# The first feed-forward's gate and up products in the 512-column form that the second one has

## The chip, the core and the metric

The kernel runs on one core of a Trainium2 chip, in one launch. Its time is the time of that core in microseconds (us): the median of three runs was 1943.56 us (1940.8 to 1944.72). The engines: TensorE (PE in the profile; PEld is its weight load), VectorE (DVE), ScalarE (ACT), GpSimd (POOL), and SyncE (SP), which issues the transfers.

## The reference, cut to what matters

The program is a four-layer model on 256 tokens with 1024 features in float32. Only the feed-forward of the first layer is touched. With `x` the normed and modulated hidden state (256 tokens by 1024), it computes

```python
a = silu(x @ w_gate) * (x @ w_up)      # 1024 -> 2816 (FFN_HIDDEN), twice
y = a @ w_down                         # 2816 -> 1024
```

and the second layer's feed-forward is the same with other weights.

## The kernel before, in words

Precision. Each float32 operand is cut into a high part (rounded to fp32r, a copy by ScalarE) and a low part (the operand minus its high part, by VectorE or GpSimd). A product is the sum of three: high times high, high weight times low x, low weight times high x. x lies transposed as `hH` and `hL`, 8 tiles of 128 features by 256 tokens; the two stand side by side in the tensor `hpair`, and `hP[:, k]` is tile k of both, 512 columns.

The weight stream. All weights come in slabs of 128 x 2048, in the order of `weight_order`; for a feed-forward that is gate i, up i, down i-1, for i from 0 to 10. SyncE loads slabs into three places of `raw`. A slab is two blocks of 1024 columns (8 weight tiles of 128 x 128). For block j, ScalarE writes the high part (`cut_hi`, L2603) and VectorE or GpSimd the low part (`cut_lo`, L1512) into a ring of three blocks, so the high cut of a block waits until TensorE has used the block three before it. In a feed-forward the blocks alternate between VectorE and GpSimd (`lo_engine`: `("V", "G")[j % 2]`). By the number that the blocks have, VectorE has the first half of each slab and GpSimd the second in the first feed-forward (its first gate slab and its last down slab have places of their own), and it is the other way round in the second.

One round i of a feed-forward (`pe_ffn`, `ve_ffn`, `se_ffn`, `ge_ffn`), each engine in its own fixed order of instructions:

- TensorE: gate i (16 tiles), up i (16 tiles), down i-1 (24 matmuls of 512 columns). In the first feed-forward a tile is three matmuls of 256 columns (`pe_mm3`, L603 to L605), and both halves of the hidden tile pair share one PSUM bank. In the second it is `pe_mm2`: one matmul of 512 columns, high weight against `hP[:, k]` (L615), and one of 256, low weight against `hH` (L616); each half of the pair has a bank of its own, with the x-high product in columns 0 to 255 and the x-low product in 256 to 511.
- ScalarE: the high cuts of the blocks that come next; `Silu` of gate i; after VectorE's product the high part of the activation (`chi`, L2924); further high cuts.
- VectorE: the low cuts; `act = silu(gate) * up` (first feed-forward L1987, reading up from PSUM; second L2014, both inputs in SBUF); the low part of the activation (`clo`, L1990). In the second feed-forward it first adds the two 256-column halves of each bank with a `tensor_reduce` (`ve_halves`, L1549), four per round.
- TensorE's down i needs chi and clo of round i; it comes one whole round later, but for down 10, which stands right behind down 9.

The modulation in pieces. The matrix of the next modulations is computed by VectorE from a stream of its own, one piece of the list `ADA` at a time: `ve_ada` is two operations over 128 x 512 (L1541, or L1538 and L1541 at the first of four), and after each fourth piece TensorE sums over partitions (`pe_ada`, L824) and VectorE copies the result (L1530). A piece stands ahead of every gate and every up, on both engines, and one more behind the activation of rounds 2, 4, 6 and 8 of the first feed-forward (`FFN_PIECES`). On TensorE, the `pe_ada` that sums waits until VectorE has finished the piece before it. In the first feed-forward TensorE's sums stand ahead of gate 1, down 1 (round 2), up 4, gate 6, up 7 and gate 9.

Of the kernel before, what the change touches and what calls it, by code (L numbers as in the profile page):

```python
# [553 lines left out]
class Net:  # L554
# [490 lines left out]
    def pe_ffn(self, e, layer):  # L1045
        m = self.m
        self.P.mark("end", f"mixer{layer}", "P")
        self.pe_norm(e, f"ffn{layer}")
        for i in range(11):
            if i == 0:  # L1050
                self.banks.order = ACC
            if layer:
                self.pe_linear_halves(e, "w_gate1", i, None if i else "ffn1")
                self.banks.order = ROT
                self.pe_linear_halves(e, "w_up1", i)
            else:
                self.pe_linear(e, "w_gate0", i, 8, 2, m.hH, m.hL, None if i else "ffn0")
                self.banks.order = ROT
                self.pe_linear(e, "w_up0", i, 8, 2, m.hH, m.hL)
            if i:  # L1060
                if layer == 0 and i in FFN_PIECES:
                    self.pe_ada(e)
                if i == 10:
                    self.pe_gate_rows(e, f"ffn{layer}_post", layer, 5)
                self.pe_down(e, layer, i - 1)
        if layer == 0:
            self.pe_ada_until(e, 1, 1)
        self.pe_down(e, layer, 10)
# [900 lines left out]
    def ve_ffn(self, e, layer):  # L1969
# [5 lines left out]
        for i in range(11):  # L1975
            s = slice(2 * (i % 2), 2 * (i % 2) + 2)
            if i == 10:
                self.ve_gate_rows(e, f"ffn{layer}_post", layer, 5, f"g_ffn_post{layer}")
            if layer:
                self.ve_act_halves(e, i)  # L1980
            else:
                self.ve_linear(e, "w_gate0", i, 8, 2, first=i == 0)
                self.ve_linear(e, "w_up0", i, 8, 2)
                e.wait_ge(*self.at("out", "w_gate0", i))
                e.wait_ge(*self.at("full", "w_up0", i))
                pu = self.banks.tile("w_up0", i)[:, 0:512].rearrange("p (a t) -> p a t", a=2)
                e.tensor_tensor(out=m.act[:, s, :], in0=m.act[:, s, :], in1=pu, op=ALU.mult).then_inc(  # L1987
                    *V(("act", 0, i), ("out", "w_up0", i)))
            e.wait_ge(*self.at("hi", f"act{layer}", i))
            e.tensor_tensor(out=m.cL[:, s, :], in0=m.act[:, s, :], in1=m.cH[:, s, :].bitcast(F32), op=ALU.subtract).then_inc(  # L1990
                *V(("lo", f"act{layer}", i)))
            if i:
                if layer == 0 and i in FFN_PIECES:
                    self.ve_ada(e)
                self.ve_cuts(e, f"w_down{layer}", 16 * i - 1)
# [2 lines left out]
        self.cut_lo(e, V, self.W.last(f"w_down{layer}", 16 * 11 - 1) + 1)  # L1998
        self.ve_junction(e, f"ffn{layer}_post", ("mix1", "mix2")[layer])

    def ve_act_halves(self, e, i):

        m, V = self.m, self.V
        s = 2 * (i % 2)
        self.ve_linear(e, "w_gate1", i, 8, 2, first=i == 0)
        for j in range(2):
            self.ve_halves(e, m.act[:, s + j, :], "w_gate1", i, j)
        self.ve_linear(e, "w_up1", i, 8, 2)
        for j in range(2):
            self.ve_halves(e, m.up[:, j, :], "w_up1", i, j)  # L2010
        e.wait_ge(*V.last)
        self.cut_lo(e, V, self.W.last("w_up1", 16 * i + 15) + 3)
        e.wait_ge(*self.at("silu", 1, i))
        e.tensor_tensor(out=m.act[:, s:s + 2, :], in0=m.act[:, s:s + 2, :], in1=m.up, op=ALU.mult).then_inc(*V(("act", 1, i)))  # L2014

    def ve_mix1(self, e):
        m, V = self.m, self.V
# [881 lines left out]
    def se_ffn(self, e, layer):  # L2899
# [6 lines left out]
        for i in range(11):  # L2906
            s = slice(2 * (i % 2), 2 * (i % 2) + 2)
            self.se_linear(e, f"w_gate{layer}", i, 8, 2)
            if layer:
                self.cut_hi(e, self.W.last("w_up1", 16 * i + 15) + 1)  # L2910
                e.wait_ge(*self.at("out", "w_gate1", i, 1))
                e.activation(m.act[:, s, :], m.act[:, s, :], ACT.Silu, scale=1.0).then_inc(*A(("silu", 1, i)))
                self.cut_hi(e, self.W.last("w_up1", 16 * i + 15) + 3)
            else:
                self.se_linear(e, "w_up0", i, 8, 2)
                e.wait_ge(*self.at("full", "w_gate0", i))
                if i >= 2:
                    e.wait_ge(*self.at("lo", "act0", i - 2))
                e.activation(m.act[:, s, :], self.banks.tile("w_gate0", i)[:, :].rearrange("p (a t) -> p a t", a=2),
                             ACT.Silu, scale=1.0).then_inc(*A(("out", "w_gate0", i)))  # L2920
            e.wait_ge(*self.at("act", layer, i))
            if i >= 2:
                e.wait_ge(*self.at("down", layer, i - 2))
            e.activation(m.cH[:, s, :], m.act[:, s, :], ACT.Copy, scale=1.0).then_inc(*A(("hi", f"act{layer}", i)))  # L2924
            if i:
                self.se_cuts(e, f"w_down{layer}", 16 * i - 1)
# [710 lines left out]
```

## Time and profile before

| | value |
|---|---|
| median of three runs | 1943.56 us |
| the profiled execution's own time | 1943.31 us |
| its span | 1941.1 us |
| TensorE busy | 1867.3 us, 96% of the span |
| VectorE busy | 1442.8 us, 74% |
| ScalarE busy | 991.3 us, 51% |
| GpSimd busy | 257.8 us, 13% |
| transfer of a piece (`ada`), from issue to landing | 4.7 us |
| granted TensorE clock, mean over the span | 0.995 |
| first feed-forward, from its first gate matmul on | from 234.5 us |
| second feed-forward, the same | from 663.5 us |

The profile is of one execution. "Busy" is the time in which an engine has at least one instruction under way. Matmuls overlap in their pipeline, so the time of a stream of matmuls is read from the distance of their starts and not from their durations.

### The profile page before, as it was taken

To read this page: it belongs to the slowest core of one execution; us is meant where nothing else is said; L and a number is where in the kernel's file an instruction comes from. 1 tells how busy PE (TensorE), PEld (TensorE's weight loads), DVE (VectorE), ACT (ScalarE), POOL (GpSimd) and SP (SyncE) were. 2 spreads that over 40 slices of the span, in tenths; PEclk is the share of its full clock that TensorE was granted. 3 is DMA by queue.
4 is the path that set the end of the run, shared out by engine and by line. 5 is a ranking of instruction groups with operands and counts; after the bars stand their busy time and mean duration, and the time that the engine had idled before them with its cause. 6 is when DMAs were issued, how large, how long until landed. Compare 5 with 4: busy or idle time off the path is not lost.

```text
span 1941.1 us, 31807 instructions
## 1 busy us (share of the span) xinstructions
PE 1867.3 (96%) x12460; PEld 1688.7 (87%) x12460; DVE 1442.8 (74%) x2603; ACT 991.3 (51%) x1428; POOL 257.8 (13%) x118
## 2 busy tenths in 40 slices
PE   6999999999998999999999899999999999999998
PEld 5987799999987788889988899999988888888887
DVE  5898875568769775567666579888878887777776
ACT  5655544455455644465555555666643334444444
POOL 0001044430001244420000373000000000000000
PEclk9999999999999999999999999999999999999999
DMA  8763476756574365555344344677766765464452
GB/s 318 241 217 135 149 265 249 259 205 232 181 256 165 123 229 179 191 178 206 143 159 168 120 163 163 200 215 216 217 240 249 281 239 217 179 249 180 186 205 109
DMA packets 94548, 391.89 MB, mean 202 GB/s; under 512 B 7680, under 2 KB 41776, under 8 KB 56000
## 3 DMA queue, kind: packets, MB, share of 16 engines
q1 hardware_dynamic: 94112, 389.59, 56.7%
q8 instruction: 100, 1.64, 0.3%
q14 instruction: 48, 0.39, 0.1%
q10 hardware_dynamic: 288, 0.26, 0.0%
HBM read 371.74 MB, written 15.73 MB: 200 GB/s over the span
## 4 chain that ended last, share of the span: by engine, by line
PE 75%; DVE 14%; ACT 2%; issue 2%; DMA 1%; POOL 0%; DVEq 0%; ACTq 0%
PE ps L615 9%; PE acc L599 9%; PE acc L601 9%; PE acc L600 9%; PE ps L616 5%; PE ps L603 5%; PE ps L604 5%; PE ps L605 5%; PE acc L603 3%; PE acc L604 3%; PE acc L605 3%; DVE wlo L1512 2%; DVE arena L1541 2%; PE acc L1467 1%; PE ps L1467 1%
## 5 line engine op out<-in xcount | busy, mean ns | idle before, releaser
L2603 ACT ACTIVATE whi<-raw 128x1024 fp32r<-128x1024 f32 x553 | 584.2, 1059 | 427.4 <-PE acc L601 206.1
L1512 DVE TENSOR_TENSOR wlo<-raw,whi 128x1024 fp32r<-128x1024 f32 x457 | 556.3, 1224 | 276.0 <-ACT whi L2603 275.6
L1512 POOL TENSOR_TENSOR wlo<-raw,whi 128x1024 fp32r<-128x1024 f32 x96 | 240.0, 2503 | 605.5 <-ACT whi L2603 605.2
L599 PE MATMUL acc<-whi,chi 128*128 128x512 f32 x744 | 293.9, 395 | 4.3 <-DVE wlo L1512 1.9
L601 PE MATMUL acc<-wlo,chi 128*128 128x512 f32 x744 | 291.2, 391 | 0.0
L600 PE MATMUL acc<-whi,clo 128*128 128x512 f32 x744 | 290.5, 390 | 0.0
L615 PE MATMUL ps<-hpair,whi 128*128 128x512 f32 x784 | 278.8, 397 | 1.4 <-POOL wlo L1512 1.4
L603 PE MATMUL ps<-hpair,whi 128*128 128x256 f32 x912 | 262.8, 288 | 4.3 <-DVE wlo L1512 3.1
L604 PE MATMUL ps<-hpair,whi 128*128 128x256 f32 x912 | 258.6, 284 | 0.0
L605 PE MATMUL ps<-hpair,wlo 128*128 128x256 f32 x912 | 258.5, 283 | 0.0
L616 PE MATMUL ps<-hpair,wlo 128*128 128x256 f32 x784 | 219.8, 280 | 0.0
L603 PE MATMUL acc<-hpair,whi 128*128 128x256 f32 x712 | 205.3, 288 | 4.3 <-DVE wlo L1512 3.6
L604 PE MATMUL acc<-hpair,whi 128*128 128x256 f32 x712 | 201.3, 283 | 0.0
L605 PE MATMUL acc<-hpair,wlo 128*128 128x256 f32 x712 | 201.3, 283 | 0.0
L603 PEld LDWEIGHTS ps<-hpair,whi 128*128 128x128 f32 x912 | 175.4, 192 | 6.4 <-issue 2.6
L615 PEld LDWEIGHTS ps<-hpair,whi 128*128 128x128 f32 x784 | 147.3, 188 | 36.9 <-issue 1.6
L604 PEld LDWEIGHTS ps<-hpair,whi 128*128 128x128 f32 x912 | 175.5, 192 | 0.3
L605 PEld LDWEIGHTS ps<-hpair,wlo 128*128 128x128 f32 x912 | 175.3, 192 | 0.0
L599 PEld LDWEIGHTS acc<-whi,chi 128*128 128x128 f32 x744 | 140.1, 188 | 36.0 <-issue 2.7
L601 PEld LDWEIGHTS acc<-wlo,chi 128*128 128x128 f32 x744 | 139.9, 188 | 31.6
L600 PEld LDWEIGHTS acc<-whi,clo 128*128 128x128 f32 x744 | 140.3, 189 | 26.8
L616 PEld LDWEIGHTS ps<-hpair,wlo 128*128 128x128 f32 x784 | 147.9, 189 | 2.5
(509 smaller groups left out, 3101.4 us busy)
## 6 DMA issues: line engine op xcount, KB each, us to landing
raw<-in_peer_down SPq DMA_DIRECT2D x64, 1024.0 KB, 4.9
raw<-in_peer_up SPq DMA_DIRECT2D x64, 1024.0 KB, 5.0
arena<-in_ada SPq DMA_DIRECT2D x80, 512.0 KB, 4.7
raw<-in_w_gate SPq DMA_DIRECT2D x22, 1024.0 KB, 4.8
raw<-in_w_up SPq DMA_DIRECT2D x22, 1024.0 KB, 4.9
raw<-in_w_down SPq DMA_DIRECT2D x22, 1024.0 KB, 4.8
arena<-spill SPq DMA_DIRECT2D x14, 1024.0 KB, 6.8
spill<-hT_t SPq DMA_DIRECT2D x22, 448.0 KB, 6.3
```

Of the source, the lines that this page charges most:

```text
L599: e.matmul(out, xh, hi, start=start, stop=False, skip_group_check=True)
L600: e.matmul(out, xl, hi, start=False, stop=False, skip_group_check=True)
L601: i = e.matmul(out, xh, lo, start=False, stop=stop, skip_group_check=True)
L603: e.matmul(out, hi, xh, start=start, stop=False, skip_group_check=True)
L604: e.matmul(out, hi, xl, start=False, stop=False, skip_group_check=True)
L605: i = e.matmul(out, lo, xh, start=False, stop=stop, skip_group_check=True)
L615: e.matmul(ps.rearrange("p (s t) -> p s t", s=2), hi, self.m.hP[:, k], start=k == 0, stop=False, skip_group_check=True)
L616: i = e.matmul(ps[:, 0:T], lo, self.m.hH[:, k, :], start=False, stop=k == 7, skip_group_check=True)
L1467: t = e.matmul(ps[:, i * 128:(i + 1) * 128], m.oh1[:, n % 3, i * 128:(i + 1) * 128], m.oh2[n % 3][:, i * 128:(i + 1) * 128], start=True, s ...
L1512: e.tensor_tensor(out=lo, in0=w, in1=hi.bitcast(F32), op=ALU.subtract).then_inc(*X(("lo", j)))
L1541: e.scalar_tensor_tensor(out=m.ada_acc, in0=w, scalar=c, in1=m.ada_acc, op0=ALU.mult, op1=ALU.add).then_inc(*V(*([("ada", s)] if k else [])))
L2603: e.activation(hi, w, ACT.Copy, scale=1.0).then_inc(*self.A(("hi", j)))
```

## The change

The first feed-forward takes the second's form. In `pe_ffn` both layers call `pe_linear_halves`. VectorE's `ve_act_halves` gets the layer as an argument: per round it adds the two gate banks into `act`, does its piece and its low cuts, adds the two up banks into `up`, makes the low cuts up to three blocks past up's last one (before: two, and no cut between up's sum and the product), waits for ScalarE's Silu, and multiplies `act` by `up`, both in SBUF. ScalarE cuts high parts up to one block past up's last, then waits for VectorE's sum of the gate, applies Silu in SBUF, cuts two blocks more, and waits for the product.

```diff
@@ pe_ffn
-            if layer:
-                self.pe_linear_halves(e, "w_gate1", i, None if i else "ffn1")
-                self.banks.order = ROT
-                self.pe_linear_halves(e, "w_up1", i)
-            else:
-                self.pe_linear(e, "w_gate0", i, 8, 2, m.hH, m.hL, None if i else "ffn0")
-                self.banks.order = ROT
-                self.pe_linear(e, "w_up0", i, 8, 2, m.hH, m.hL)
+            self.pe_linear_halves(e, f"w_gate{layer}", i, None if i else f"ffn{layer}")
+            self.banks.order = ROT
+            self.pe_linear_halves(e, f"w_up{layer}", i)
@@ ve_ffn
-            if layer:
-                self.ve_act_halves(e, i)
-            else:
-                self.ve_linear(e, "w_gate0", i, 8, 2, first=i == 0)
-                self.ve_linear(e, "w_up0", i, 8, 2)
-                e.wait_ge(*self.at("out", "w_gate0", i))
-                e.wait_ge(*self.at("full", "w_up0", i))
-                pu = self.banks.tile("w_up0", i)[:, 0:512].rearrange("p (a t) -> p a t", a=2)
-                e.tensor_tensor(out=m.act[:, s, :], in0=m.act[:, s, :], in1=pu, op=ALU.mult).then_inc(
-                    *V(("act", 0, i), ("out", "w_up0", i)))
+            self.ve_act_halves(e, layer, i)
@@ ve_act_halves, with the layer for the 1 in every name
+        self.ve_linear(e, f"w_gate{layer}", i, 8, 2, first=i == 0)
         for j in range(2):
+            self.ve_halves(e, m.act[:, s + j, :], f"w_gate{layer}", i, j)
+        self.ve_linear(e, f"w_up{layer}", i, 8, 2)
         for j in range(2):
+            self.ve_halves(e, m.up[:, j, :], f"w_up{layer}", i, j)
+        e.wait_ge(*V.last)
+        self.cut_lo(e, V, self.W.last(f"w_up{layer}", 16 * i + 15) + 3)
+        e.wait_ge(*self.at("silu", layer, i))
+        e.tensor_tensor(out=m.act[:, s:s + 2, :], in0=m.act[:, s:s + 2, :], in1=m.up, op=ALU.mult).then_inc(*V(("act", layer, i)))
@@ se_ffn
-            if layer:
-                self.cut_hi(e, self.W.last("w_up1", 16 * i + 15) + 1)
-                e.wait_ge(*self.at("out", "w_gate1", i, 1))
-                e.activation(m.act[:, s, :], m.act[:, s, :], ACT.Silu, scale=1.0).then_inc(*A(("silu", 1, i)))
-                self.cut_hi(e, self.W.last("w_up1", 16 * i + 15) + 3)
-            else:
-                self.se_linear(e, "w_up0", i, 8, 2)
-                e.wait_ge(*self.at("full", "w_gate0", i))
-                if i >= 2:
-                    e.wait_ge(*self.at("lo", "act0", i - 2))
-                e.activation(m.act[:, s, :], self.banks.tile("w_gate0", i)[:, :].rearrange("p (a t) -> p a t", a=2),
-                             ACT.Silu, scale=1.0).then_inc(*A(("out", "w_gate0", i)))
+            self.cut_hi(e, self.W.last(f"w_up{layer}", 16 * i + 15) + 1)
+            e.wait_ge(*self.at("out", f"w_gate{layer}", i, 1))
+            e.activation(m.act[:, s, :], m.act[:, s, :], ACT.Silu, scale=1.0).then_inc(*A(("silu", layer, i)))
+            self.cut_hi(e, self.W.last(f"w_up{layer}", 16 * i + 15) + 3)
```

## Rows read from the trace of the kernel before

**Rows 1.** The page: the chain that ended last, by engine.

```profile
PE 75%; DVE 14%; ACT 2%; issue 2%; DMA 1%; POOL 0%; DVEq 0%; ACTq 0%
```

**Rows 2.** Windows: length, PE, PEld, DVE, ACT, POOL busy (instructions), clock, DMA share, GB/s.

```profile
250.03:419.39 169.36, 169.29 (x1221) 160.51 (x1220) 103.48 (x105) 71.60 (x78) 74.71 (x29) 1.00 0.72 259
679.64:842.60 162.96, 162.96 (x869) 139.51 (x869) 97.68 (x100) 72.25 (x78) 70.51 (x29) 1.00 0.56 198
```

**Rows 3.** Timeline of PE: start, us, engine, line, operation; ends of two gapless streams.

```profile
338.27 0.28 PE L603 MATMUL ps<-hpair,whi 128*128 128x256 f32 x1
...
343.55 0.28 PE L605 MATMUL ps<-hpair,wlo 128*128 128x256 f32 x1
...
747.07 0.40 PE L615 MATMUL ps<-hpair,whi 128*128 128x512 f32 x1
...
755.91 0.40 PE L615 MATMUL ps<-hpair,whi 128*128 128x512 f32 x1
```

**Rows 4.** Timeline, all engines, around the activation of round 8, first feed-forward.

```profile
384.54 0.69 DVE L1987 TENSOR_TENSOR arena<-arena,ps 128x512 f32<-128x512 f32 x1 [3.45 <-PE ps L605]
385.26 0.63 ACT L2924 ACTIVATE chi<-arena 128x512 fp32r<-128x512 f32 x1 [2.07 <-DVE arena L1987]
385.80 1.05 ACT L2603 ACTIVATE whi<-raw 128x1024 fp32r<-128x1024 f32 x1
385.93 0.69 DVE L1990 TENSOR_TENSOR clo<-arena,chi 128x512 fp32r<-128x512 f32 x1 [0.70 <-ACT chi L2924]
386.73 1.54 DVE L1541 SCALAR_TENSOR_TENSOR arena<-arena,gs_t 128x512 f32<-128x512 f32 x2
387.28 1.06 ACT L2603 ACTIVATE whi<-raw 128x1024 fp32r<-128x1024 f32 x1 [0.43 <-PE acc L601]
388.42 3.22 POOL L1512 TENSOR_TENSOR wlo<-raw,whi 128x1024 fp32r<-128x1024 f32 x1 [3.22 <-ACT whi L2603]
389.74 1.05 PE L824 MATMUL ps<-kc_t,arena 128*128 128x128 f32 x8
390.00 1.06 ACT L2603 ACTIVATE whi<-raw 128x1024 fp32r<-128x1024 f32 x1 [1.66 <-PE acc L601]
```

**Rows 5.** Timeline of DVE and POOL: a piece that meets a GpSimd cut.

```profile
300.65 3.56 DVE L1541 SCALAR_TENSOR_TENSOR arena<-arena,gs_t 128x512 f32<-128x512 f32 x2
300.86 2.80 POOL L1512 TENSOR_TENSOR wlo<-raw,whi 128x1024 fp32r<-128x1024 f32 x1 [3.22 <-ACT whi L2603]
```

**Rows 6.** Timeline of the first feed-forward's start: DVE, POOL, ACT, PE.

```profile
241.63 7.34 DVE L1541 SCALAR_TENSOR_TENSOR arena<-arena,gs_t 128x512 f32<-128x512 f32 x4
246.02 2.40 POOL L1512 TENSOR_TENSOR wlo<-raw,whi 128x1024 fp32r<-128x1024 f32 x1 [0.60 <-ACT whi L2603]
244.88 1.06 ACT L2603 ACTIVATE whi<-raw 128x1024 fp32r<-128x1024 f32 x1 [1.07 <-PE ps L605]
245.47 0.38 PE L603 MATMUL ps<-hpair,whi 128*128 128x256 f32 x1 [0.69 <-POOL wlo L1512]
249.02 1.16 PE L824 MATMUL ps<-kc_t,arena 128*128 128x128 f32 x8 [0.42 <-DVE arena L1541]
```

**Rows 7.** Timeline of the first feed-forward's end: last product, cuts, down 9, down 10.

```profile
419.12 1.03 PE L769 MATMUL ps<-kc_t,gs_t 128*128 128x128 f32 x8
420.65 1.04 ACT L2603 ACTIVATE whi<-raw 128x1024 fp32r<-128x1024 f32 x1
421.73 1.23 DVE L1512 TENSOR_TENSOR wlo<-raw,whi 128x1024 fp32r<-128x1024 f32 x1 [0.26 <-ACT whi L2603]
422.87 1.22 DVE L1512 TENSOR_TENSOR clo<-raw,chi 128x1024 fp32r<-128x1024 f32 x1
424.15 0.50 PE L599 MATMUL acc<-chi 128*128 128x512 f32 x1
```

**Rows 8.** The second feed-forward: a pair of sums, and a product that meets GpSimd.

```profile
678.33 1.28 DVE L1549 TENSOR_REDUCE arena<-ps 128x256 f32<-128x512 f32 x2
679.64 2.57 DVE L2014 TENSOR_TENSOR arena<-arena 128x512 f32<-128x512 f32 x1
```

More of the change, by code:

```diff
@@ L1999, in ve_ffn, with ve_act_halves @@
         self.ve_junction(e, f"ffn{layer}_post", ("mix1", "mix2")[layer])
-    def ve_act_halves(self, e, i):
+    def ve_act_halves(self, e, layer, i):
         m, V = self.m, self.V
         s = 2 * (i % 2)
-        self.ve_linear(e, "w_gate1", i, 8, 2, first=i == 0)
+        self.ve_linear(e, f"w_gate{layer}", i, 8, 2, first=i == 0)
         for j in range(2):
-            self.ve_halves(e, m.act[:, s + j, :], "w_gate1", i, j)
-        self.ve_linear(e, "w_up1", i, 8, 2)
+            self.ve_halves(e, m.act[:, s + j, :], f"w_gate{layer}", i, j)
+        self.ve_linear(e, f"w_up{layer}", i, 8, 2)
         for j in range(2):
-            self.ve_halves(e, m.up[:, j, :], "w_up1", i, j)
+            self.ve_halves(e, m.up[:, j, :], f"w_up{layer}", i, j)
         e.wait_ge(*V.last)
-        self.cut_lo(e, V, self.W.last("w_up1", 16 * i + 15) + 3)
-        e.wait_ge(*self.at("silu", 1, i))
-        e.tensor_tensor(out=m.act[:, s:s + 2, :], in0=m.act[:, s:s + 2, :], in1=m.up, op=ALU.mult).then_inc(*V(("act", 1, i)))
+        self.cut_lo(e, V, self.W.last(f"w_up{layer}", 16 * i + 15) + 3)
+        e.wait_ge(*self.at("silu", layer, i))
+        e.tensor_tensor(out=m.act[:, s:s + 2, :], in0=m.act[:, s:s + 2, :], in1=m.up, op=ALU.mult).then_inc(*V(("act", layer, i)))
     def ve_mix1(self, e):
```

## The prediction

> **What bounds the kernel now.** I read the chain of waits first: TensorE holds 75% of what ended last [rows 1]. Then the windows from the first product of each feed-forward to its last [rows 2]: in the first one TensorE is busy for 169.29 of 169.36 us, so the stage is as long as its matmuls. Whatever VectorE gets to do is free until a wait of TensorE appears, and a saving is worth what it takes out of TensorE's stream. The second feed-forward, which has the new form, needs 162.96 us for the same work. That gap of 6.4 us is not the gain: besides cheaper tiles, the first holds sums of the modulation (L824), five in its window, which stay (1.05 us long each, 389.74 in [rows 4]; 4 to 5 us in all). So the distances of matmul starts come next [rows 3], and last the timelines of one round, of the start and of the end [rows 4 to 7], to see which waits the new order makes.
>
> **Matmuls removed and added.** Before, from 338.27 to 343.55 there are 44 steps of 256 columns: 0.1200 us each, 0.3600 us a tile. In the second feed-forward, from 747.07 to 755.91 there are 25 tiles of 512 + 256 columns: 0.3536 us each [rows 3]. The columns are the same 768; one instruction and one weight load go. Each tile saves 0.0064 us. Of 11 x 32 = 352 tiles, the 16 of gate 0 go through `pe_first`, with the same matmuls in both forms; 336 x 0.0064 = 2.15 us saved. Bounds: 1.7 to 2.2, the lower one from the windows [rows 2], where what is left after the down matmuls and sums is about 0.360 against 0.355 us a tile.
>
> The Trainium skill ("TensorE: Matmul & The Clock Gate", Back-to-back issue gap) gives the isolated gap at full clock as N / 2.4 + 2.5 ns, so that one instruction less saves 2.5 ns a tile, an estimate of 0.84 us over 336 tiles. The rows show 6.4 ns, and a step of 256 columns 11 ns longer than that formula's; the sum by it would be 1.3 us later.
>
> **VectorE's additions.** Four reduces a round at 0.64 us (1.28 for two, [rows 8]) are 2.56 us, 28 us in all. The window shows VectorE busy 103.5 of 169.4 us, so there is room; the price lies only where somebody waits for it. Below, U is the start of the first matmul behind up (the product L1987 starts at U + 0.27; in round 8 U = 384.27), and T' the start of the next gate, or of a sum ahead of it: 389.74, so U + 5.47 [rows 4].
>
> In round i the new order on VectorE behind U is: second reduce of up at U + 0.27 to 0.95; then the low cut of the next gate's first half, which now stands before the product. ScalarE's high cut of that block can start when up's last block is used, U + 0.26 (as 390.00 follows 389.74), and VectorE's low cut starts 1.08 behind a high cut's start (420.65 to 421.73), so U + 1.34; the product follows 1.14 later (421.73 to 422.87), U + 2.48. That is 2.2 us later than today. The rest keeps the steps of [rows 4]: chi 0.72 behind (U + 3.20), clo 0.67 behind chi (3.87), ScalarE's high cut of the next gate's second half 0.54 behind chi (3.74), GpSimd's low cut of it 1.14 behind (4.88), and a piece of the modulation 0.80 behind clo (4.67). Nobody on TensorE waits for chi and clo, but for round 10. GpSimd's cut, 2.80 us when a piece meets it [rows 5], ends at U + 7.7. TensorE wants it 2.83 behind T' (8 tiles), at U + 8.3 less a load ahead: 0.45 us to spare. I cost it at nothing; if the cover goes, see the second rival.
>
> What meets what: an L1541 that is issued while GpSimd cuts ends 0.55 us behind GpSimd (300.65 + 3.56 = 304.21 against 300.86 + 2.80 = 303.66, [rows 5]). The first operation of the piece starts at 4.67, ahead of GpSimd; the second is caught and ends at 7.68 + 0.55 = U + 8.23. Today in round 8 the piece runs 386.73 to 388.27, ahead of GpSimd's 388.42 [rows 4].
>
> - Rounds 2, 4, 6, 8 have a piece behind the activation. Behind round 8's, TensorE's sum ahead of gate 9 waits for exactly that piece (`pe_ada` waits for the piece before). It could start at U + 5.47 and gets it at U + 8.29: **2.8 us of new stall**, once. The other sums have a piece before them that was done long before: in round 2 and at up 4 and up 7 half a slab's tiles or more earlier, at gate 6 the piece of up 5.
> - Rounds 4 and 6: the gate's own piece follows, 1.54 us for two operations [rows 4], then the low cut of the next up's first half (1.22 us), from 8.23 + 1.54 = U + 9.8 to 11.0. TensorE wants it at T' + 5.66 less a load ahead, U + 11.0. Together 0.2 us lost; bounds 0 and 2, the latter if each slips by a sum's length. In round 2 TensorE's own sum shifts T' by up to 1 us and there is room.
> - Bank waits: gate and up now take four banks of four a round; each is needed again a round later, and its reduce is done in U + 0.95 at the latest. Nothing, lower bound and upper.
> - Transfers: slabs free with the low cuts; GpSimd's, which frees the gate slab, comes 0.7 us later (U + 4.88 against 388.42 - 384.27 = 4.15), against a slab every 5.5 us or so. The pieces' own transfers wait for VectorE two pieces back and take 4.7 us; ahead of up 5 and up 7 VectorE may wait for one until about 1 us later, with 0.9 us of room behind. Nothing, up to 1 us.
>
> **The start.** Today TensorE's sum ahead of gate 1 waits 0.42 us in its row and some more before: up 0 restarts at 245.47 and needs 16 - 8 = 8 tiles, to 248.3, but the sum starts at 249.02, because the fourth L1541 was issued at 246.00, just as GpSimd took 246.02 to 248.42 [rows 6]. In the new order ScalarE does Silu (after two operations of the piece, 241.63 + 1.54, two reduces, to 244.4, and a table load that ends about 245.1) before the high cut that is at 244.88 today; the cut moves to about 245.6, GpSimd to 246.75, and the L1541 gets through by 246.75. **0.7 us saved**, bounds 0 (caught again) and 0.7.
>
> **The end.** Down 10 stands right behind down 9, and its last weight block has a place in `chi`'s memory: high cut behind chi, low cut behind clo. Today the matmul that uses it starts at 424.15, U + 5.03, right behind that low cut (422.87 + 1.22 = 424.09, [rows 7]). Now chi is at U + 3.20, the high cut of the spare at 3.74, the low cut at 4.82 to 6.04; the matmul at U + 6.1: **1.05 us lost**, not covered by anything, since the junction behind it waits for the accumulators. Bounds 0.7 and 2.4, the latter if the product is caught by GpSimd.
>
> **Sum.** -2.15 - 0.7 + 2.8 + 0.2 + 1.05 = +1.2 us. On the profiled execution's own 1943.31 us (span 1941.1 and 2.2 around it) that is 1944.5. That execution is 0.25 us under the median 1943.56, so for a median I write 1944.7. The gain in the stream is real and is spent on three waits.
>
> **Rivals.**
> 1. *No new stall*: GpSimd's cut is later or the piece sooner, so the sum ahead of gate 9 finds its piece done, and the end costs little. For it: the second feed-forward does run gapless in this form [rows 2]; against: there, but for the first two rounds, no pieces are left, and it is GpSimd that has the next gate's first half, so that VectorE's product comes 1 us behind U. Time: 1943.6 - 2.15 - 0.7 = 1940.7.
> 2. *GpSimd's cut misses the gate's second half every round.* The new product has both inputs in SBUF and took 2.57 us with GpSimd busy, against 0.69 [rows 8, 4]. If in each round it is caught at U + 2.5, chi and GpSimd's next cut come up to 1.9 us later, which passes the 0.45 us of room: 1.4 us in each of 9 rounds, 13 us, 1956. It decides from the point where GpSimd is still cutting at U + 2.5. Against: GpSimd's cut before that follows the use of up's first half, U - 2.83 + 0.26 + 1.14 = U - 1.4, and takes 2.4 [rows 6], so it ends at U + 1.0. The Trainium skill ("SBUF — State Buffer", Who interferes with whom) says that a VectorE instruction with two SBUF inputs and a GpSimd one that reads SBUF exclude each other for the whole instruction, and a `tensor_reduce` never contends; the trace agrees (2.57 us for the product, reduces at 0.64 beside GpSimd). By that rule alone every product would be exposed that was not before, with the time just given.
> 3. *Rounds 4 and 6 (and the transfers of pieces) slip as well*: +2 to 3 us more, 1947.
>
> **How the numbers follow.** Forecast 60% (its own range 1943 to 1946.5), rival 1 20%, rival 2 (in whole or in part, 1948 to 1957) 12%, rival 3 8%. 0.2% is 3.9 us, about what a measurement of this kernel can tell from no change: faster means below 1939.7, slower above 1947.4. Faster takes savings at their upper bounds, no stall, and 1 us besides: 5%. Slower: rival 2 and a third of rival 3: 15%. The rest, 80%, is no change. The range leaves out rival 2 and a part of rival 1: 1940.5 to 1948.5.
>
> **What would show it.** In the changed kernel's profile: L615 and L616 at 0.3536 us a tile in the first stage; no L1987; L2014 about 2.5 us behind the first down matmul in rounds 1 to 9, at 0.69 us; L824 ahead of gate 9 with an idle of TensorE of about 2.8 us before it, released by L1541; L824 ahead of gate 1 with none; the spare block's matmul about 6.1 us behind the last up matmul. Wrong would be: TensorE idle ahead of the second half of gates (rival 2), or no idle at gate 9 (rival 1).

## The result, and the profile after

The change costs 0.46%: 1950.96 us (six runs, 1948.38 to 1953.25) against 1941.52 us (six runs, 1939.65 to 1944.72), a ratio of 1.0046 with a 95% interval of 1.0034 to 1.0057. The forecast was 1944.7 us, with a range up to 1948.5; it was +1.2 us on the median of three then known (1943.56), against +9.4 us here. The profiled execution of the changed kernel took 1953.25 us, its span 1951.4 us. In the rows below, line numbers before L1512 are unchanged, `cut_lo` is now L1507, `ve_ada` L1536, `ve_halves` L1544, `clo` L1976, the product L2000, `cut_hi` L2589, `chi` L2902 and Silu L2897.

The page after: the chain that ended last by engine, the gate and up matmuls among its costliest groups (busy us, mean ns of one | idle ahead of them, and what ended most of it), and the busy times of the engines.

```profile
PE 75%; DVE 14%; ACT 3%; issue 2%; DMA 1%; POOL 0%; DVEq 0%; ACTq 0%; SPq 0%
...
L615 PE MATMUL ps<-hpair,whi 128*128 128x512 f32 x1120 | 401.0, 400 | 5.6 <-DVE wlo L1507 3.4
...
PE 1870.0 (96%) x12124; PEld 1672.6 (86%) x12124; DVE 1469.1 (75%) x2647; ACT 992.1 (51%) x1428; POOL 256.9 (13%) x118
```

By engine, the chain stands almost as it did [rows 1]. The difference is in the idle: 5.6 us ahead of L615, most of it released by a low cut of VectorE. The window from the first product to the last of the first feed-forward, with the columns of [rows 2], puts it in place:

```profile
250.21:427.41 177.20, 171.18 (x903) 146.22 (x902) 131.22 (x146) 72.36 (x78) 73.58 (x29) 0.98 0.67 245
```

In the window of the first feed-forward TensorE now idles 177.20 - 171.18 = 6.02 us, where it idled 0.07 us, and the granted clock is 0.98. Whoever waited for whom is in the waits of TensorE between 234 and 450 us (total, times, longest):

```profile
PE ps L615 <- DVE wlo L1507: 3.4, 2, 2.1
PE ps L824 <- DVE arena L1536: 2.6, 1, 2.6
PE acc L599 <- ACT chi L2902: 1.0, 1, 1.0
PE ps L615 <- POOL wlo L1507: 0.9, 1, 0.9
```

The stage, from the first transpose (L757) of the norm ahead of this feed-forward to the first of the norm behind it, is 202.93 us before and 210.81 after: +7.88 us. To see which rounds pay, I cut the stage where the down products begin: the first matmul of L599 behind up i (for round 10 that is 0.8 us behind U below, since eight matmuls of L769 stand between). "1" is from the start of the stage to the first down matmul of round 1, the other numbers are from the first down matmul of the round before, so that "5" has gate 5 and up 5 in it, and "end" is from that of round 10 to the end of the stage. In every row the parts add up to the stage, but for rounding.

```
us            1      2      3      4      5      6      7      8      9      10     end    stage
before        29.96  17.79  17.08  17.87  16.98  17.87  17.86  16.98  17.87  17.77  14.90  202.93
after         28.72  17.81  16.85  17.58  20.61  17.46  19.14  16.76  22.17  17.58  16.13  210.81
e1            29.14  17.60  16.86  17.58  16.76  17.50  21.80  16.75  18.84  17.58  17.21  207.62
e2            28.74  17.65  16.85  17.58  17.58  17.44  18.43  16.76  17.50  17.56  16.13  202.22
e3            28.72  17.80  16.86  17.58  19.12  17.46  19.14  16.74  17.58  21.63  16.13  208.77
e4            28.75  17.65  16.83  17.58  19.14  17.44  19.05  16.76  22.86  17.56  16.13  209.73
e5            28.78  17.60  16.86  17.58  16.76  17.50  17.56  16.76  19.26  17.55  14.77  200.97
e6            28.56  17.57  16.86  17.58  16.76  17.50  17.56  16.76  17.50  17.56  14.72  198.91
e7            28.71  17.81  16.85  17.58  20.64  17.46  19.04  16.77  20.62  17.55  16.13  209.17
```

An undisturbed round without a sum (round 8) is 16.76 us now and was 16.98: 0.22 us less, the price of 32 tiles at 0.0069 us. Rounds 5, 7 and 9 are 3.6, 1.3 and 4.3 us longer than before, and the end 1.2 us. Round 9 and the end are what the prediction named; rounds 5 and 7 it had at 0.2 us together.

A text written ahead of a run that names a step from one activation to the next takes it from `clo` to `clo`; so measured, round 9 of the changed kernel is 22.53 us. Where `clo` itself moves within its round the two measures differ, by up to 2.7 us.

**Round 9.** The timeline around the activation of round 8, all engines, as [rows 4]:

```profile
387.30 1.23 DVE L1507 TENSOR_TENSOR wlo<-raw,whi 128x1024 fp32r<-128x1024 f32 x1 [0.53 <-ACT whi L2589]
388.45 0.69 DVE L2000 TENSOR_TENSOR arena<-arena 128x512 f32<-128x512 f32 x1
...
389.83 0.69 DVE L1976 TENSOR_TENSOR clo<-arena,chi 128x512 fp32r<-128x512 f32 x1 [0.70 <-ACT chi L2902]
390.63 3.50 DVE L1536 SCALAR_TENSOR_TENSOR arena<-arena,gs_t 128x512 f32<-128x512 f32 x2
390.83 2.76 POOL L1507 TENSOR_TENSOR wlo<-raw,whi 128x1024 fp32r<-128x1024 f32 x1 [3.98 <-ACT whi L2589]
...
394.19 1.65 PE L824 MATMUL ps<-kc_t,arena 128*128 128x128 f32 x8 [2.65 <-DVE arena L1536]
```

The last up matmul before it is followed by down at 385.88 (U). The cut now stands ahead of the product (387.30, 388.45), so `clo` is at U + 3.95 and the piece at U + 4.75, 0.20 us ahead of GpSimd's cut. Its second operation is caught, meaning that it was issued while GpSimd was cutting and ended only behind that cut: the piece ends at 394.13, 0.54 us behind GpSimd, and TensorE's sum starts at U + 8.31, forecast at U + 8.29.

**Rounds 5 and 7.** The timeline of gate 5, DVE, POOL and PE:

```profile
311.92 0.39 PE L599 MATMUL acc<-whi,chi 128*128 128x512 f32 x1
...
316.66 5.19 DVE L1536 SCALAR_TENSOR_TENSOR arena<-arena,gs_t 128x512 f32<-128x512 f32 x4
321.59 2.50 POOL L1507 TENSOR_TENSOR wlo<-raw,whi 128x1024 fp32r<-128x1024 f32 x1 [1.93 <-ACT whi L2589]
321.77 3.40 DVE L1507 TENSOR_TENSOR wlo<-raw,whi 128x1024 fp32r<-128x1024 f32 x1
325.31 0.47 PE L615 MATMUL ps<-hpair,whi 128*128 128x512 f32 x1 [2.13 <-DVE wlo L1507]
```

The first row is the first matmul behind up 4, so U = 311.92. Two pieces run back to back (4 operations, 5.19 us). Between U and the end of the cut VectorE's waits are put down to up's last matmul, ScalarE's high cut and `chi`, none to a transfer. VectorE's low cut of up's first half is issued behind them, 0.18 us after GpSimd took its own cut, and lasts 3.40 us instead of 1.22: it ends 1.08 us behind GpSimd, and TensorE, which wants it for the first tile of up 5, stands for 2.13 us. In the kernel before, the same cut was issued at 323.22, 1.10 us ahead of GpSimd:

```profile
323.22 1.22 DVE L1512 TENSOR_TENSOR wlo<-raw,whi 128x1024 fp32r<-128x1024 f32 x1
...
324.32 2.40 POOL L1512 TENSOR_TENSOR wlo<-raw,whi 128x1024 fp32r<-128x1024 f32 x1 [2.35 <-ACT whi L2603]
```

Gate 7 has the same pair of rows again in the changed kernel (3.40 us issued at 359.85, GpSimd at 359.67), with an idle of 1.24 us; there TensorE still has the sum ahead of up 7 to do.

**The clock.** Windows of 2 us behind gate 5's stall and gate 9's (columns as above; the clock is the number ahead of the last two):

```profile
325.00:327.00 2.00, 1.69 (x8) 1.49 (x9) 1.90 (x4) 0.60 (x1) 0.00 (x0) 0.86 1.05 389
327.00:329.00 2.00, 2.00 (x8) 1.71 (x7) 1.96 (x3) 0.03 (x1) 0.00 (x0) 0.50 1.01 426
329.00:331.00 2.00, 2.00 (x10) 1.75 (x10) 0.83 (x2) 1.05 (x1) 0.00 (x0) 0.79 0.09 37
...
395.00:397.00 2.00, 2.00 (x9) 1.81 (x9) 1.09 (x3) 0.00 (x0) 0.00 (x0) 0.50 0.95 324
397.00:399.00 2.00, 2.00 (x10) 1.71 (x10) 1.36 (x2) 0.00 (x0) 0.00 (x0) 0.72 1.04 434
```

After TensorE had stood still, the granted clock went from 1.00 to 0.50 (2.4 to 1.2 GHz) for about 3.4 us, although TensorE was busy again. A window at 0.50 holds 8 or 9 matmuls; the same tiles at 1.00 are 14 (the second window of e7 below). Time times missing share is 1.7 us for each fall. This is not in the prediction's sum at all.

**Start and end.** The stage begins 0.93 us earlier in the trace of after (230.95, before 231.88). At the start (timeline of ACT, POOL and PE), Silu now stands ahead of the high cut, so GpSimd's cut, at 245.85 for 246.02 before, is 0.76 us later by the stage's own time, and the sum ahead of gate 1 has no idle before it (0.42 us in [rows 6]):

```profile
244.19 0.63 ACT L2897 ACTIVATE arena<-arena 128x512 f32<-128x512 f32 x1
245.85 3.35 POOL L1507 TENSOR_TENSOR wlo<-raw,whi 128x1024 fp32r<-128x1024 f32 x1 [1.37 <-ACT whi L2589]
247.48 1.05 PE L824 MATMUL ps<-kc_t,arena 128*128 128x128 f32 x8
```

At the end the last up matmul is followed at U = 424.85. TensorE waits for `chi`, and the matmul on the spare weight block comes at 431.03, U + 6.2 (forecast U + 6.1, before U + 5.03 [rows 7]):

```profile
429.58 0.47 PE L599 MATMUL acc<-whi,chi 128*128 128x512 f32 x1 [0.96 <-ACT chi L2902]
...
429.74 1.22 DVE L1507 TENSOR_TENSOR clo<-raw,chi 128x1024 fp32r<-128x1024 f32 x1 [0.25 <-ACT chi L2589]
...
431.03 0.49 PE L599 MATMUL acc<-chi 128*128 128x512 f32 x1
```

### The profile page after: what moved, and what is told of

Same layout as the page of the kernel before. It is cut to its first block, busy times and chain, and to the rows that moved or that the text cites. A ratio compares the mean times of both kernels' runs of the same rounds, so it can differ in the third digit from the quotient of the medians.

```text
span 1951.4 us, 31192 instructions
## 1 busy us (share of the span) xinstructions
PE 1870.0 (96%) x12124; PEld 1672.6 (86%) x12124; DVE 1469.1 (75%) x2647; ACT 992.1 (51%) x1428; POOL 256.9 (13%) x118
## 4 chain that ended last, share of the span: by engine, by line
PE 75%; DVE 14%; ACT 3%; issue 2%; DMA 1%; POOL 0%; DVEq 0%; ACTq 0%; SPq 0%
PE ps L615 13%; PE acc L599 9%; PE acc L601 9%; PE acc L600 9%; PE ps L616 6%; PE acc L603 3%; PE acc L604 3%; PE acc L605 3%; PE ps L603 3%; PE ps L604 3%; PE ps L605 3%; DVE wlo L1507 3%; DVE arena L1536 2%; PE acc L1462 1%; PE ps L1462 1%
## 5 line engine op out<-in xcount | busy, mean ns | idle before, releaser
L2589 ACT ACTIVATE whi<-raw 128x1024 fp32r<-128x1024 f32 x553 | 583.9, 1059 | 426.8 <-PE acc L601 187.8
L1507 DVE TENSOR_TENSOR wlo<-raw,whi 128x1024 fp32r<-128x1024 f32 x457 | 561.7, 1235 | 269.7 <-ACT whi L2589 269.2
L615 PE MATMUL ps<-hpair,whi 128*128 128x512 f32 x1120 | 401.0, 400 | 5.6 <-DVE wlo L1507 3.4
L1507 POOL TENSOR_TENSOR wlo<-raw,whi 128x1024 fp32r<-128x1024 f32 x96 | 239.7, 2499 | 615.0 <-ACT whi L2589 614.8
L599 PE MATMUL acc<-whi,chi 128*128 128x512 f32 x744 | 294.6, 396 | 5.6 <-DVE wlo L1507 1.9
L615 PEld LDWEIGHTS ps<-hpair,whi 128*128 128x128 f32 x1120 | 211.7, 189 | 57.5 <-DVE wlo L1507 3.8
L616 PEld LDWEIGHTS ps<-hpair,wlo 128*128 128x128 f32 x1120 | 212.7, 190 | 2.8
L599 PEld LDWEIGHTS acc<-whi,chi 128*128 128x128 f32 x744 | 140.3, 189 | 38.9 <-issue 2.8
L603 PE MATMUL ps<-hpair,whi 128*128 128x256 f32 x576 | 166.4, 289 | 3.7 <-DVE wlo L1507 3.3
L604 PE MATMUL ps<-hpair,whi 128*128 128x256 f32 x576 | 162.8, 283 | 0.0
L1536 DVE SCALAR_TENSOR_TENSOR arena<-arena,gs_t 128x512 f32<-128x512 f32 x140 | 131.4, 938 | 15.1 <-DMA arena<-in_ada 6.5
L603 PEld LDWEIGHTS acc<-hpair,whi 128*128 128x128 f32 x712 | 136.3, 191 | 7.1 <-ACT whi L2589 2.6
L604 PEld LDWEIGHTS acc<-hpair,whi 128*128 128x128 f32 x712 | 136.5, 192 | 0.0
```

The lines of the kernel that those rows point to most:

```text
L599: e.matmul(out, xh, hi, start=start, stop=False, skip_group_check=True)
L603: e.matmul(out, hi, xh, start=start, stop=False, skip_group_check=True)
L604: e.matmul(out, hi, xl, start=False, stop=False, skip_group_check=True)
L615: e.matmul(ps.rearrange("p (s t) -> p s t", s=2), hi, self.m.hP[:, k], start=k == 0, stop=False, skip_group_check=True)
L616: i = e.matmul(ps[:, 0:T], lo, self.m.hH[:, k, :], start=False, stop=k == 7, skip_group_check=True)
L1507: e.tensor_tensor(out=lo, in0=w, in1=hi.bitcast(F32), op=ALU.subtract).then_inc(*X(("lo", j)))
```

## The experiments

**Theory.** The stage pays for two collisions of VectorE with GpSimd's low cut: the piece behind round 8's activation (gate 9), and the low cut of up's first half behind two pieces (gates 5 and 7); some of the idles bring a fall of the clock, which costs again. Both collisions come from the order of VectorE's instructions behind up: cut, product, `clo`, piece. **Rivals:** VectorE simply has too much to do, so that any order stalls; the stalls come from transfers; the extra time is the clock's alone. Times before, for the first four kernels 1943.55 us (22 runs), for the others 1943.53 us (29 runs); ratios are to these, each with its 95% interval.

**e1: GpSimd gets the first half of each slab, VectorE the second, as in the second feed-forward.**

```diff
-            return ("V", "G")[j % 2]
+            return ("V", "G")[(j + (name[-1] == "0")) % 2]
```

> The changed kernel, with the halves of the first feed-forward's slabs exchanged: GpSimd cuts the first half, VectorE the second, as in the second feed-forward. Theory A (the loss is a matter of what stands next to what: VectorE operations caught behind a GpSimd cut ahead of gate 9 and behind gates 5 and 7, with the TensorE clock that falls in two of these stalls, and the late product at the end): no low cut stands before the product, so the product comes 1.5 us sooner, the extra piece runs at about 4.5 to 6.0 us behind up, the sum ahead of gate 9 waits 0.6 us instead of 2.65, and the low cuts behind gates 5 and 7 start before GpSimd's; up to 1 us is lost at the end and 0.5 at the start. First stage 7 to 9 us shorter than in the changed kernel, median 1941 to 1944. Theory B (the form itself costs, by reduces, banks or the product in SBUF): no change from the changed kernel, 1951.

Measured: 1949.11 us, 1.0035 [1.0023, 1.0047]; the stage is 207.62 us. A miss. The timeline of POOL and DVE at gate 7 shows that one collision was exchanged for another:

```profile
345.48 2.40 POOL L1507 TENSOR_TENSOR wlo<-raw,whi 128x1024 fp32r<-128x1024 f32 x1 [2.81 <-ACT whi L2589]
345.60 2.83 DVE L2000 TENSOR_TENSOR arena<-arena 128x512 f32<-128x512 f32 x1
...
351.07 2.62 POOL L1507 TENSOR_TENSOR wlo<-raw,whi 128x1024 fp32r<-128x1024 f32 x1 [3.19 <-ACT whi L2589]
351.38 3.40 DVE L1507 TENSOR_TENSOR wlo<-raw,whi 128x1024 fp32r<-128x1024 f32 x1
```

Here the product itself is issued 0.12 us behind GpSimd (rival 2's mechanism in the prediction), and 5.8 us later the low cut as well. In this run the product is caught in seven of the eleven rounds, at 2.22 to 2.90 us. The last time, at the end of the stage, TensorE waits 2.04 us for `chi`, where the changed kernel waits 0.96. The second feed-forward has the same assignment without such stalls; there no pieces stand after its first rounds, so the assignment of the halves alone is not what keeps it free.

**e2: the piece of rounds 2, 4, 6, 8 moved ahead of the cut and the product.**

```diff
@@ ve_act_halves, behind the two sums of up
+        if layer == 0 and i in FFN_PIECES:
+            self.ve_ada(e)
         e.wait_ge(*V.last)
@@ ve_ffn, behind clo
-                if layer == 0 and i in FFN_PIECES:
-                    self.ve_ada(e)
```

> The changed kernel, with VectorE's extra piece of rounds 2, 4, 6 and 8 moved from behind the activation's low part to ahead of the product. Theory A: the piece runs at about 1 to 2.5 us behind up, when GpSimd is idle; the sum ahead of gate 9 finds it done (its 3.0 us gap and the 1.5 us of half clock behind it go), and the gate pieces of rounds 5 and 7 no longer push the low cut behind GpSimd's (another 5.3 us); GpSimd's cut of the next gate's second half comes 1.3 us later in four rounds and costs up to 0.4 us each. Sum 8 us less than the changed kernel: 1942 to 1944.5. Theory B: 1951, the same number of operations on the same engines.

Measured: 1943.44 us, 0.9997 [0.9987, 1.0007]; stage 202.22 us. The stall at gate 9 is gone (round 9: 17.50 us) and so are the caught low cuts. Gates 5 and 7 keep idles of 0.59 and 0.58 us instead of 2.13 and 1.24, now for GpSimd's cut, which the later product delays (rounds 5 and 7: 17.58 and 18.43 us). The work on VectorE is the same. That speaks against the rival of too much work: the order alone is worth 8.6 us of the stage, two falls of the clock among them. It also speaks against transfers, of which it removes none, as do VectorE's waits in round 5 of the changed kernel. An idle of 0.95 us at the end is left as well.

**e3: the last piece behind round 9 instead of round 8.**

```diff
-FFN_PIECES = (2, 4, 6, 8)
+FFN_PIECES = (2, 4, 6, 9)
```

> The changed kernel, with the extra pieces in rounds 2, 4, 6 and 9 instead of 2, 4, 6 and 8. Theory A: the sum that comes behind 8 is now at up 9, far from the piece before it, so the gap of 3.0 us ahead of gate 9 and the half clock behind it go (4.5 us), but four operations in a row now stand ahead of the low cut in round 10, which is caught behind GpSimd's as in rounds 5 and 7 (1.3 to 3.8 us back). 1948 to 1950. If the caught low cuts were not the cause in rounds 5 and 7, round 10 gives nothing back and it is 1946.5.

Measured: 1948.35 us, 1.0027 [1.0015, 1.0039]; stage 208.77 us. Round 9 takes 17.58 us instead of 22.17, 4.6 us less than in the changed kernel: the wait and the clock fall behind it both go with the piece. Round 10 now takes 21.63 us instead of 17.58, with a fall of the clock in it. Its gate has the second collision at a place where it had not been (timeline of POOL, DVE, PE):

```profile
409.59 2.69 POOL L1507 TENSOR_TENSOR wlo<-raw,whi 128x1024 fp32r<-128x1024 f32 x1 [1.93 <-ACT whi L2589]
409.97 3.40 DVE L1507 TENSOR_TENSOR wlo<-raw,whi 128x1024 fp32r<-128x1024 f32 x1
413.52 0.47 PE L615 MATMUL ps<-hpair,whi 128*128 128x512 f32 x1 [2.33 <-DVE wlo L1507]
```

So a piece behind the activation and then the gate's own piece make the collision in round 10 as they do in rounds 5 and 7.

**e4 and e7: TensorE given matmuls of no use ahead of the sum of gate 9**, into the next bank, 24 in e4 and 13 in e7. They change nothing of the result; they fill the idle.

```diff
@@ pe_linear_halves, ahead of pe_ada
+        if (name, i) == ("w_gate0", 9):
+            self.pe_fill(e, 24)
...
+    def pe_fill(self, e, n):
+        b = self.banks.order[self.banks.turn % 4]
+        e.wait_ge(*self.at("out", *self.banks.holds[b]))
+        for _ in range(n):
+            e.matmul(self.banks.tiles[b][:, 0:128], self.m.ones, self.m.kc_t[:, 0:128], start=True, stop=True, ...)
```

> The changed kernel, with 24 matmuls of 128 columns (ones, into the bank that the sum takes next) in the wait ahead of gate 9, about 2.8 us of them. Theory A: the wait for VectorE stays, TensorE just works in it; if it is the idle time that lets the clock fall, the granted clock stays at 1.00 in the tiles behind it and the gate's tiles take 0.354 us from the first on: 1.5 us less than the changed kernel. If the fall has another cause (the slow stretch would come anyway), the clock falls to 0.5 all the same and the time is that of the changed kernel or a little more.

> As the fill ahead of gate 9, with 13 matmuls instead of 24, which took 5.35 us and so outlasted the wait they were to fill (13 make 2.9 us). If the clock falls because TensorE idles, the sum starts as late as in the changed kernel (3.0 us behind the last down matmul), the clock stays at 1.00 and gate 9's tiles take 0.354 us from the first: the step from the activation of round 8 to that of round 9 is 20.8 to 21.0 us instead of 22.53. If not, 22.5.

Measured: e4 1950.68 us, 1.0040 [1.0026, 1.0054], stage 209.73 us. The clock stayed at 1.00 behind gate 9, but the 24 matmuls stand in the trace as 48, and they outlasted the wait (timeline of PE; L742 is the filling, L834 the sum, since the edit shifts the lines by ten):

```profile
389.50 5.52 PE L742 MATMUL ps<-kc_t 128*128 128x128 f32 x48
394.85 1.06 PE L834 MATMUL ps<-kc_t,arena 128*128 128x128 f32 x8
```

So round 9 is 22.86 us, longer than in the changed kernel. The clock did what was expected and the time did not, so this run tells nothing of the fall's price. With half as many in e7 the filling ends inside the wait, and the windows behind it stay at 1.00:

```profile
389.12 3.06 PE L742 MATMUL ps<-kc_t 128*128 128x128 f32 x26
392.02 1.08 PE L834 MATMUL ps<-kc_t,arena 128*128 128x128 f32 x8
```

```profile
392.00:394.00 2.00, 2.00 (x17) 1.87 (x16) 0.82 (x3) 0.00 (x0) 0.00 (x0) 1.00 0.46 143
394.00:396.00 2.00, 2.00 (x14) 1.72 (x13) 1.66 (x3) 0.00 (x0) 0.00 (x0) 1.00 1.06 430
```

Measured: e7 1947.28 us, 1.0020 [1.0010, 1.0029], stage 209.17 us; round 9 is 20.62 us against 22.17 (from `clo` to `clo`, 20.97 against 22.53), so that the fall behind gate 9 is worth about 1.6 us. The rest, 20.62 - 17.58 (round 9 of e3, with a sum and no wait) = 3.0 us, is mostly the wait of 2.8 us.

**e5: the low cut moved behind the product.**

```diff
         e.wait_ge(*V.last)
-        self.cut_lo(e, V, self.W.last(f"w_up{layer}", 16 * i + 15) + 3)
         e.wait_ge(*self.at("silu", layer, i))
         e.tensor_tensor(out=m.act[:, s:s + 2, :], ...).then_inc(*V(("act", layer, i)))
+        self.cut_lo(e, V, self.W.last(f"w_up{layer}", 16 * i + 15) + 3)
```

> The changed kernel, with VectorE's low cut of the next gate's first half moved from before the product to right behind it (the extra pieces stay behind the activation). Theory A: the product comes 1.2 to 1.5 us sooner in every round, and with it chi, ScalarE's next high cut and GpSimd's. The low cuts behind gates 5 and 7 then start before GpSimd's (their stalls of 3.8 and 1.5 us go), the end loses nothing (1.3 us go), but the extra piece of round 8 is still caught behind GpSimd's cut: the wait ahead of gate 9 stays at about 2 us idle, with or without the half clock behind it. 5 to 7.5 us less than the changed kernel, 0.5 to 3 us over the kernel before. If the place of that one cut is not what delays the others, the stage stays at 210 to 211 us.

Measured: 1940.60 us, 0.9986 [0.9977, 0.9995]; stage 200.97 us. A miss: the time is below before, where it was expected above. Timeline of DVE, POOL and PE at gates 5 and 9:

```profile
315.69 5.27 DVE L1536 SCALAR_TENSOR_TENSOR arena<-arena,gs_t 128x512 f32<-128x512 f32 x4
320.88 1.22 DVE L1507 TENSOR_TENSOR wlo<-raw,whi 128x1024 fp32r<-128x1024 f32 x1
321.91 2.44 POOL L1507 TENSOR_TENSOR wlo<-raw,whi 128x1024 fp32r<-128x1024 f32 x1 [3.14 <-ACT whi L2589]
...
384.26 3.65 DVE L1536 SCALAR_TENSOR_TENSOR arena<-arena,gs_t 128x512 f32<-128x512 f32 x2
387.96 1.16 PE L824 MATMUL ps<-kc_t,arena 128*128 128x128 f32 x8 [1.50 <-DVE arena L1536]
```

The low cut of up's first half stands 1.03 us ahead of GpSimd and takes 1.22 us; the stalls of gates 5 and 7 and of the end are gone (rounds 5 and 7 are 16.76 and 17.56 us, the end 14.77). At gate 9 the piece is still caught and 1.50 us of idle is left, with no fall of the clock behind it. That is what the expectation missed: the idle is 1.15 us shorter than in the changed kernel where about 2 us were expected, and the fall is gone too.

**e6: both, the piece ahead of the product and the cut behind it.** The diff is e2's and e5's together.

> The changed kernel with both: the extra piece ahead of the product and the low cut of the next gate behind it. Theory A: no stall is left but the one at the start (0.87 us); the first stage shows the whole of the matmuls' saving, 200 to 200.5 us against 202.9 before and 202.2 with the piece moved alone: 2.4 to 2.8 us less than the kernel before, ratio 0.9986. If the form of the product cost something of its own, the stage would stay above 202.

Measured: 1939.57 us, 0.9984 [0.9976, 0.9993]; stage 198.91 us, 4.02 us less than before. The stage was expected at 200 to 200.5 us, so it is over 1 us shorter than that; the median, 3.96 us below before, agrees with the stage. It is the lowest median of all kernels here; by time alone it can't be told from e5 (1940.60 us, the intervals overlap), by the stage it is 2.05 us shorter. In the feed-forward TensorE has one idle left above 0.3 us, 0.86 us at its start, so this run shows what the cheaper matmuls are worth when nothing spends them: more than the prediction had (below). In round 8 (timeline of DVE, POOL, PE) the piece is over 2.4 us before GpSimd starts, and the sum waits for nobody:

```profile
380.14 1.54 DVE L1536 SCALAR_TENSOR_TENSOR arena<-arena,gs_t 128x512 f32<-128x512 f32 x2
...
382.32 1.22 DVE L1507 TENSOR_TENSOR wlo<-raw,whi 128x1024 fp32r<-128x1024 f32 x1
384.10 2.38 POOL L1507 TENSOR_TENSOR wlo<-raw,whi 128x1024 fp32r<-128x1024 f32 x1 [3.99 <-ACT whi L2589]
384.65 1.05 PE L824 MATMUL ps<-kc_t,arena 128*128 128x128 f32 x8
```

**c0: the kernel before once more**, for how far two profiles of the same code differ.

> The kernel before, profiled once more: how much of a difference between two profiles is there without any change. The first stage should be 202.9 us within 0.1; the later stages should differ by where the TensorE clock falls: 0 to 4 us over the span, as the changed kernel's profile shows three falls between its two feed-forwards and that of before shows one. If the later stages always need 226.0 and 1082.9 us in this kernel, the 2.4 and 0.7 us that the changed kernel's profile loses there belong to the change.

Measured: 1942.66 us, span 1940.5 us. The stage is 202.92 us against 202.93, and the rounds agree within 0.02 us: without a fall of the clock in it this stage repeats to a few hundredths. Between the feed-forwards the profiles of all kernels have falls of the clock. A window of 2 us of the kernel before, and one of its repetition, with TensorE busy for the whole of either:

```profile
590.00:592.00 2.00, 2.00 (x17) 1.58 (x14) 1.37 (x7) 1.26 (x2) 2.00 (x4) 0.60 1.04 414
```

```profile
600.00:602.00 2.00, 2.00 (x15) 1.68 (x13) 0.79 (x2) 0.33 (x1) 0.00 (x0) 0.50 0.80 233
```

The clock lost there (time times missing share) is 1.7 us in these two, in e1 and in e7, 3.4 in e3, and 5.1 in the changed kernel, e2, e4, e5 and e6. So it differs between kernels with the same code in that part, and I read stage lengths and the medians and not the spans. Whether the new form has more of these falls than the old one is not settled by two profiles of the old and eight of the new. The span of the changed kernel is 10.3 us longer than before, of which the stage has 7.88 us, and 2.4 us lie behind it up to the second feed-forward.

## Why the prediction was wrong

Its steps against the changed kernel's stage, in us. For a wait the measure is the gap between matmul starts less the usual gap.

```
step of the prediction                        forecast   measured
tiles, 336 x 0.0064                            -2.15      -2.8    (336 x 0.0084, below)
start, sum ahead of gate 1                     -0.7       -0.55   (below)
wait ahead of gate 9                           +2.8       +2.8    (gap 3.03 against 0.23)
clock behind gate 9                             none      +1.6    (22.17 - 20.62, e7)
rounds 4 and 6 (gates 5 and 7)                 +0.2       +5.4    (20.61 - 16.76 and 19.14 - 17.56, e6)
end                                            +1.05      +1.2    (16.13 - 14.90)
sum                                            +1.2       +7.65   (the stage: +7.88)
```

**What held.** The start: its step and round 2 together are 46.53 us for 47.75 before, 1.22 us less, of which 80 tiles at 0.0084 us are 0.67; 0.55 is left for the start. The product came at U + 2.6 (rounds 4 and 8) and took 0.68 to 0.69 us in all eleven rounds, so rival 2 was rightly not in the sum. In one stretch the distance of matmul starts is as forecast: 31 tiles of the changed kernel (timeline of PE, first and last of a gapless stream) stand 10.60 us apart over 30 steps, 0.3533 us each.

```profile
374.93 0.40 PE L615 MATMUL ps<-hpair,whi 128*128 128x512 f32 x1
...
385.53 0.40 PE L615 MATMUL ps<-hpair,whi 128*128 128x512 f32 x1
```

In another, behind the sum ahead of gate 6, it is 9.70 us over 28 steps, 0.3464 us each:

```profile
339.93 0.39 PE L615 MATMUL ps<-hpair,whi 128*128 128x512 f32 x1
...
349.63 0.39 PE L615 MATMUL ps<-hpair,whi 128*128 128x512 f32 x1
```

So a tile saves 6.7 or 13.6 ns against 0.3600, by the stretch, and the forecast had taken only the smaller of the two. Over the undisturbed rounds 3, 4, 6, 8 and 10 it is 1.34 us for 160 tiles, 0.0084 us each; e6 has 2.42 us for 288 tiles, the same. Why the distance differs was not looked into. The Trainium skill ("TensorE: Matmul & The Clock Gate", Back-to-back issue gap) would have given 2.5 ns an instruction less, so here the rows were right to go by.

The piece behind round 8 was forecast at U + 4.67 to U + 8.23 and came at U + 4.75 to U + 8.25; e2 and e3 showed that this piece and the order that delays it make the stall. The end moved by the spare block's low cut, U + 6.2 for a forecast of U + 6.1, and e5 and e6 took it away by moving that cut.

**The step that failed** is "Rounds 4 and 6 ... Together 0.2 us lost". The time of issue was right: U + 9.8 forecast, 321.77 - 311.92 = U + 9.85 measured. What was wrong is the 1.22 us. I asked of the product and of the pieces whether GpSimd would be cutting when they are issued, and not of the low cuts, because in the trace of before none of them had met GpSimd (up's first half stood at U + 8.64, ahead of it). GpSimd's next cut follows the same gate, 321.59 = U + 9.67; so at U + 9.8 a low cut is caught until 1.08 us behind its end, and takes 3.40 us. It ends at U + 13.25 for a need at U + 11.0, and TensorE idles 2.13 us. Gate 7 does the same with a smaller idle, 1.24 us. e5 tests exactly this (the cut at U + 8.65, 1.2 us earlier: 1.22 us, no stall), and e3 makes the same stall at a new gate. The forecast's upper bound, 2 us for both, was made from a slip of 1 us each, which has no collision in it. Rival 3 named the place, with 1947, but as a slip and not as a cut that is caught; rival 2, whose mechanism this is, put it on the product alone.

**What no step had** is the clock. Behind gate 9 the fall is worth about 1.6 us (e7 against the changed kernel), and behind gate 5 about the same: round 5 is 20.61 and 20.64 us where the clock fell (changed kernel, e7) and 19.12 and 19.14 us where it did not (e3, e4), with the same code up to there and an idle of 2.13 or 2.14 us in all four. So whether the fall comes is not fixed by the code, and its price is 1.5 us when it does. Of idles in this stage with a fall behind them there are 2.13, 2.13, 2.33, 2.38 and 2.65 us; without one, 2.04, 2.13, 2.14 and all the shorter ones. Outside the stage the length decides as little: an idle of 1.9 us at 203 to 206 us had a fall behind it in c0, e2, e4 and e5 and none in the other six, and one of 3.24 us (e1, at 602.33) had none. What decides stays open.

The stage is 7.88 us longer in the profiles and the medians differ by 9.4 us. The 1.6 us between them are within what the reference's median moves: 1941.52 us in the six runs beside the changed kernel, 1943.55 and 1943.53 us in the 22 and 29 beside the experiments. The mean granted clock of the six runs of the changed kernel is 0.9935, that of the 22 of before 0.9950, and 0.0015 of 1950 us is 2.9 us of clock. That fits two more falls in the other runs too, but it does not show them: e1, with one fall in the stage of its profile, has a mean of 0.9933.

## What to carry to other kernels

When an edit moves an instruction on a vector engine, list every instruction behind it up to the next wait of TensorE, and ask of each, also of those that have never been late, whether the other engine's long cut will be under way at the new time of issue: here 1.2 us of delay turned 1.22 us into 3.40. An engine that is 75% busy can be made to stall at three places or at none by its order alone, so the cheaper matmuls were only worth having with the cut behind the product (1940.60 us), and most with the piece ahead of it as well (1939.57 us, and a stage 4.0 us shorter than before). A stall of about 2 us in a stream of matmuls should be priced at up to 1.6 us more than its length, for the clock behind it.

## What the runs showed of the hardware

- A low cut on VectorE (two inputs in SBUF) that is issued 0.18 to 0.38 us behind GpSimd's cut takes 3.40 us instead of 1.22 and ends about 1.1 us behind it; the same with the product (2.83 instead of 0.69 us in e1). The sums of two PSUM halves (L1544) stayed at 0.69 us: of the 44 in the changed kernel's stage 25 lie wholly inside a cut of GpSimd, and none took longer. The Trainium skill ("SBUF — State Buffer", Who interferes with whom) states this rule, that such a pair excludes each other for the whole instruction while a `tensor_reduce` never contends, and the traces agree.
- GpSimd pays too, where VectorE's operation came first. In the changed kernel's stage its cut took 2.37 to 2.41 us with no such operation under way at its issue, 2.50 us with 0.26 us of a piece's operation left (321.59), 2.76 to 2.81 us with 0.55 us left (390.83), and 3.35 us with 1.1 us of a low cut left (245.85).
- The granted clock fell to 0.50 behind some idles of TensorE and not behind others as long; with matmuls of no use in the idle ahead of gate 9 it stayed at 1.00 behind it (e4, e7).
- A pair of a 512-column and a 256-column matmul takes 0.3533 us in some gapless stretches and 0.3464 us in others of the same kernel, both at a granted clock of 1.00.
- Falls of the clock between the feed-forwards, where the code is the same in all kernels, cost 1.7 us in some profiles, 3.4 us in one and 5.1 us in others.
